# Third mixer: attention probabilities turned by a product with diag(1/sum)

## The chip, the cores and the metric

The kernel runs on one core of a Trainium2 chip. What is measured is the device time of one execution in microseconds; of several runs the median is shown. Beside it there is one execution with the hardware profiler, from which the profile and the trace come.

## What is computed

Two blocks of two layers each over 256 context tokens and 256 latent tokens of width 1024, in float32. The four mixers are, in order: gated linear attention beside softmax attention, a gated recurrence, latent attention beside retention (the third mixer, which the change touches), and a state-space scan; each is followed by a feed-forward part. The attention of the third mixer, with 8 heads:

```python
def attend(q, k, v):
    s = jnp.einsum('bqhd,bkhd->bhqk', q, k).astype(jnp.float32) * (QK_DIM ** -0.5)
    p = jax.nn.softmax(s, axis=-1).astype(v.dtype)
    return jnp.einsum('bhqk,bkhd->bqhd', p, v)

# in mla_retention_mixer: latent queries see context and latent keys, context queries the context alone
    q_c, k_c, v_c = mla_heads(z_c[..., :MLA_IN], ...)
    q_l, k_l, v_l = mla_heads(z_l[..., :MLA_IN], ...)
    a_l = blocked_attend(q_l, concat(k_c, k_l), concat(v_c, v_l))      # blocks of 128 queries
    a_c = attend(q_c, k_c, v_c)
    y = concatenate([a, r]) @ w_out                                     # r is the retention
```

## The kernel before

The program is written by hand: each engine has its own list of stages and runs through it in order, and semaphores (`wait_ge`, `then_inc`) tie them. Three helpers carry most operations, so most rows of the profile have their lines: `Pe.mm` (L169, a matmul with stationary `w` and moving `x`; `ps<-x,w` in the profile's names), `Pe.tr` (L179, TensorE's transpose, moving the identity that stands in `sb_cst`), and `Vec.tt` (L200, a product or sum of two tensors on VectorE or GpSimd). ScalarE's copies are L258, its exponentials with a row sum L253, other activations L252; VectorE's maxima are L229, its small scalings L214, reciprocals L226, scaled products L217.

The third mixer is the class `Mla`. After its projections it runs 23 steps. In each step stand side by side: one attention unit in four phases, the making of a query or key head (with its norm and its rotation) for a later unit, a part of the retention, and a part of the modulation vectors of a later stage (`mods`, with weights by DMA, `ps<-sb_slot,sb_SX`). Each engine goes through its part of a step in a fixed order, so what is queued earlier in a step holds back what is queued later.

An attention unit is two heads by 128 queries. There are 16: for each pair of heads m, c = 0 and 1 are context queries with nk = 256 keys, c = 2 and 3 latent queries with nk = 512. Unit u = 4m + c. The class `Attend` has its phases:

- TensorE, `scores` in step s: two matmuls into banks 3 and 4. VectorE, `maxima`. ScalarE, `exps`: P = exp(scale * s - max) into SBUF, with the row sums in r.
- VectorE, `norms`, later in step s: rr = 1/r, then P = P * rr, one product over both heads, 128 x 2nk elements; it signals "pn".
- TensorE, `turn`, in step s+1, head by head: waits for "pn" and for its bank, and turns the nk/128 blocks of P into bank 5 with the identity. There is one bank for the turns, so head 1 waits until ScalarE has copied head 0 to PT (`copies`). Between the two turns TensorE does `values` of the unit before.
- TensorE, `values`, in step s+2: v times PT into bank 6; ScalarE, `gather`, copies the bank after c = 3.

TensorE's order in a step is: turn of head 0, values of the older unit, turn of head 1, scores of the next unit, a part of mods, rotation, the new head's product, retention, the head's sum of squares, a part of mods. P and PT have two buffers each, chosen by u % 2. `Attend` is also used by the first mixer (`Even`), whose `st` holds P, PT, m and r.

`p.RA` is a buffer of 128 x 2048 floats. In the trace it is written by two transfers of modulation weights before 760 us and is used again by the state-space scan after 2034 us.

Of the kernel before, what the change touches and what calls it, by code (L numbers as in the profile page):

```python
# [16 lines left out]
D = 1024  # L17
# [70 lines left out]
class Events:  # L88
# [3 lines left out]
    def __init__(self, nc, ctx):  # L92
        self.nc, self.ctx = nc, ctx
        self.sems, self.n, self.at, self.bank, self.ends = {}, {}, {}, {}, {}
        self.counting = True
# [953 lines left out]
def block_load(W, c0):  # L1049

    view = lambda s: s[:, :].rearrange("p (k n) -> p k n", k=KT)
    return 4096, [(view, W[:, c0:c0 + 512].rearrange("(k p) n -> p k n", p=128))]
# [1112 lines left out]
class Attend:  # L2165
# [8 lines left out]
    def turn(self, pe, u, h):  # L2174
        p, tag = self.p, self.tag
        nk = self.units[u][1]
        b = self.tb[h % len(self.tb)]
        pe.wait_ge("pn", tag, u)
        pe.vacant(b)
        for j in range(nk // 128):  # L2180
            i = pe.tr(p.ps[b][:, 128 * j:128 * j + 128], self.st["P"][u % 2][:, h, 128 * j:128 * j + 128])
        i.then_inc(*pe.sig("tr", tag, u, h))
        pe.until(b, "pt", tag, u, 1 if len(self.tb) == 2 else h)

# [81 lines left out]
    def norms(self, dve, u):  # L2266
        tag, st = self.tag, self.st
        nk = self.units[u][1]
        P = st["P"][u % 2][:, :, 0:nk]
        r, rr = (st["r"][:, i, 2 * u:2 * u + 2] for i in range(2))  # L2270
        dve.wait_ge("p", tag, u, 1)
        dve.recip(rr, r).then_inc(*dve.sig("recip", tag, u))
        dve.wait_ge("recip", tag, u)
        dve.mul(P, P, rr.unsqueeze(2).broadcast_to([128, 2, nk])).then_inc(*dve.sig("pn", tag, u))


# [716 lines left out]
class Mla:  # L2993
# [7 lines left out]
    def __init__(self, p, mods, next_mods, before):  # L3001
        self.p, self.mods, self.more, self.before = p, mods, next_mods, before
        io = p.io
        W = io["w_in_2"][0]
        place = Place(p.room, 8192)
        self.rq, self.rk, self.rg, self.rv = (place(4, T) for _ in range(4))
        self.cq, self.ckv, self.kr = place(2, T), place(T), place(T)
        narrow = [(lambda s: s[:, :].rearrange("p (k n) -> p k n", k=KT)[:, :, 0:416], W[:, 0:416].rearrange("(k p) n -> p k n", p=128))]
        cp = lambda x, sc=1.0: [(x[:, m, :], ACT.Copy, sc) for m in range(4)]
        self.proj = Projections(  # L3010
            p, "mla.in", [block_load(W, 416), (4096, narrow)] + [block_load(W, c0) for c0 in (928, 1440, 1952)], mods,
            [("features", cp(self.rq)),
             ("narrow", [("features", 128 * m, 128, 0, self.cq[:, m, :]) for m in range(2)]
              + [("features", 256, 128, 0, self.ckv), ("features", 320, 96, 64, self.kr[64:96, :])]),
             ("features", cp(self.rk, 0.125)), ("tokens", cp(self.rv)),
             ("features", [(self.rg[:, m, :], ACT.Silu, 1.0) for m in range(4)])], ("ffn1.res", "x"), ("mla.in", "x"))

        top = place.at
        low = Place(p.room, 0, 8192)
        self.QH, self.KH = low(4, T), low(4, T)  # L3020
        self.su, (za, zb) = 1, p.slots[2:4]
        s = p.slots[self.su]
        self.tmps = [(low(T), low(T)), (s[:, 2560:3072], s[:, 3072:3584])]
        rt, self.t1 = s[:, 3584:3584 + TC], s[:, 3840:3968]
        self.wu, self.wk = s[:, 0:1536].rearrange("p (k n) -> p k n", k=2), s[:, 1536:2560]
        place = Place(p.room, top)
        P = [place(2, T), place(2, T), low(2, T), za[:, 2048:3072].rearrange("p (h n) -> p h n", h=2)]
        self.vv = low(4, T)
        st = {"P": P[0:2], "PT": P[2:4], "m": place(32), "r": place(2, 32)}
        self.kvnorm = RmsHeads(p, "kv", self.ckv, "ones", 128, T, 128, p.v("mkv_n"), self.tmps[0], 0, 3)  # L3030
        self.items, units = [], []
        for h in range(8):
            q, k = self.QH[0:96, h % 4, :], self.KH[0:96, h % 4, :]
            self.items += [(RmsHeads(p, (h, y), z, "ones", 96, T, 96, p.v(gain)[0:96], self.tmps[y], 0, 3),
                            Rope(p, (h, y), z[:, TC:T], 96, "rotM", "cosM", "sinM", rt, 0, 3))
                           for y, (z, gain) in enumerate(((q, "mqn"), (k, "mkn")))]
        for m, c in itertools.product(range(4), range(4)):
            nk = TC if c < 2 else T
            heads = [(self.QH[0:96, h % 4, 128 * c:128 * c + 128], self.KH[0:96, h % 4, 0:nk], lambda j, h=h: self.vv[:, j, 64 * h:64 * h + 64])
                     for h in (2 * m, 2 * m + 1)]  # L3040
            units.append((heads, nk, m, c, p.H[:, m, :] if c == 3 else None))
        self.attend = Attend(p, 0, units, 96 ** -0.5, st, (3, 4), (5,), 6)
        self.steps = len(units) + self.LAG + 2
        self.lg = place(6, 16)
        rt2 = place(TC)
        self.F, self.Rv = p.H[:, 7, :], p.H[:, 3, :]
        D = [za[:, 0:1024], za[:, 1024:2048], za[:, 3072:4096], place(1024)]
        self.DJ = [(d[:, 0:T], d[:, T:2 * T]) for d in D]
        self.o, self.r = zb[:, 3072:3072 + T], zb[:, 3584:3584 + T]
        self.ropes = [Rope(p, (n, m), x[:, m, TC:T], 128, "rotR", "cosR", "sinR", rt2, 0, 3) for n, x in enumerate((self.rq, self.rk)) for m in range(4)]  # L3050
        done = [("mla.lat", ("att", 0, m)) for m in range(4)] + [("mla.ret", ("mix", m)) for m in range(4)]
        order = (0, 4, 1, 5, 2, 6, 3, 7)
        self.out = OutProj(p, "mla", io["w_out_2"][0], p.H, 0, False, mods, order,
                           lambda e, k: e.wait_ge(*done[order[k]][1], of=done[order[k]][0]), free=self.place_free)
# [1428 lines left out]
```

## Time and profile before

| | before |
|---|---|
| median of 3 runs | 2423.95 us |
| lowest and highest | 2421.72, 2424.27 us |
| span of the profiled execution | 2417.1 us |
| TensorE busy | 2247.9 us, 93% |
| VectorE busy | 1490.4 us, 62% |
| ScalarE busy | 1083.1 us, 45% |
| attention steps of the third mixer | about 1476 to 1626 us of the span |

The profiled execution's own time is its span, from the first instruction to the last. Times in rows are microseconds unless marked ns. PE is TensorE's matmul, PEld its weight load, DVE VectorE, ACT ScalarE, POOL GpSimd. TensorE's matmuls are pipelined and their ends are modelled: several that follow each other overlap in the rows, so the time that one more costs is read from starts, not from durations. "issue" as the reason of an idle time means that no wait is visible.

### The profile page before, as it was taken

How to read it: one execution, taken by the hardware profiler on the slowest of the kernel's cores; microseconds unless marked ns; L12 is line 12 of the kernel's file. 1: busy time of each engine (PE TensorE's matmuls, PEld its weight loads, DVE VectorE, ACT ScalarE, POOL GpSimd, SP SyncE). 2: the span in 40 equal slices, each digit the busy share in tenths (PEclk: the TensorE clock that was granted, in tenths of full speed). 3: DMA queues.
4: the chain of work that ended last, by engine and by line, in shares of the span. 5: the costliest groups of instructions: out<-in, count | busy, mean ns of one | idle time of the engine just before them, and what ended most of it. 6: DMA issues, size and time to landing. Idle time of an engine off the chain costs nothing.

```text
span 2417.1 us, 35402 instructions
## 1 busy us (share of the span) xinstructions
PE 2247.9 (93%) x14822; PEld 1793.5 (74%) x14822; DVE 1490.4 (62%) x2379; ACT 1083.1 (45%) x1831; POOL 147.7 (6%) x185
## 2 busy tenths in 40 slices
PE   6978899999999999988999988989999999769999
PEld 3844476888886777777999863347888887759999
DVE  6448738565566477885457325555666566996454
ACT  4354446222234466655455435654332334545553
POOL 0001100000000000000000002200200201000210
PEclk8998999999999999998999999999999999989999
DMA  7263344344425465434553223432444434544543
GB/s 279 70 258 140 140 157 150 130 149 155 157 87 218 139 209 174 140 141 143 179 189 134 103 92 122 157 139 90 149 156 163 145 125 193 202 142 140 207 177 123
DMA packets 173439, 372.47 MB, mean 154 GB/s; under 512 B 7520, under 2 KB 99936, under 8 KB 158944
## 3 DMA queue, kind: packets, MB, share of 16 engines
q1 hardware_dynamic: 173280, 370.21, 43.9%
q8 instruction: 117, 1.92, 0.3%
q14 instruction: 42, 0.34, 0.0%
HBM read 339.74 MB, written 30.44 MB: 153 GB/s over the span
## 4 chain that ended last, share of the span: by engine, by line
PE 77%; DVE 12%; ACT 7%; issue 3%; DMA 2%; POOL 0%; SPq 0%; DVEq 0%; ACTq 0%; POOLq 0%
PE ps L169 75%; DVE sb_R L200 4%; ACT sb_R L252 2%; PE ps L179 1%; DMA sb_slot<-mod_w 1%; ACT sb_R L258 1%; DVE sb_H L200 1%; DVE sb_R L229 1%; DMA sb_slot<-even_w_in 1%; ACT L245 1%; DVE sb_R L232 1%; DVE sb_slot L200 1%; DVE sb_X L217 1%; DVE sb_WP L200 1%; DVE sb_R L214 1%
## 5 line engine op out<-in xcount | busy, mean ns | idle before, releaser
L169 PE MATMUL ps<-sb_HP,sb_WP 128*128 128x512 f32 (+1 forms) x5808 | 1070.5, 345 | 16.2 <-DVE sb_HP L200 9.9
L169 PEld LDWEIGHTS ps<-sb_HP,sb_WP 128*128 128x128 f32 x5808 | 915.8, 190 | 155.3 <-issue 16.5
L200 DVE TENSOR_TENSOR sb_WP<-sb_slot,sb_WP 128x1024 fp32r<-128x1024 f32 x380 | 467.7, 1236 | 554.4 <-ACT sb_WP L258 553.6
L258 ACT ACTIVATE sb_WP<-sb_slot 128x1024 fp32r<-128x1024 f32 x380 | 399.2, 1057 | 706.5 <-PE ps L169 680.7
L169 PE MATMUL ps<-sb_XP,sb_WP 128*128 128x256 f32 (+1 forms) x2976 | 499.1, 330 | 0.6 <-DVE sb_R L200 0.4
L169 PEld LDWEIGHTS ps<-sb_XP,sb_WP 128*128 128x128 f32 x2976 | 446.5, 190 | 52.3 <-DVE sb_R L200 0.9
L200 DVE TENSOR_TENSOR sb_R<-sb_R 128x256 f32<-128x256 f32 (+4 forms) x411 | 202.0, 527 | 12.9 <-ACT sb_R L252 10.0
L169 PE MATMUL ps<-sb_R 128*32 128x64 f32 (+7 forms) x1768 | 163.4, 292 | 35.8 <-issue 8.0
L169 PEld LDWEIGHTS ps<-sb_R 128*32 128x32 f32 (+3 forms) x1768 | 116.0, 157 | 74.7 <-issue 37.2
L200 POOL TENSOR_TENSOR sb_R<-sb_R 128x512 f32<-128x512 f32 (+1 forms) x82 | 91.0, 1136 | 774.8 <-ACT sb_R L252 774.8
L252 ACT ACTIVATE sb_R<-ps 128x512 f32<-128x512 f32 (+1 forms) x208 | 99.2, 513 | 79.7 <-PE ps L169 75.7
L252 ACT ACTIVATE sb_R<-sb_R 128x512 f32<-128x512 f32 (+5 forms) x127 | 83.6, 667 | 81.4 <-DVE sb_R L200 79.8
L258 ACT ACTIVATE sb_R<-ps 128x512 f32<-128x512 f32 (+4 forms) x163 | 69.6, 508 | 71.3 <-PE ps L169 61.3
L169 PE MATMUL ps<-sb_WP,sb_HP 128*128 128x512 f32 x384 | 88.4, 390 | 1.3 <-DVE sb_HP L200 1.3
L169 PEld LDWEIGHTS ps<-sb_WP,sb_HP 128*128 128x128 f32 x384 | 71.8, 188 | 17.3 <-DVE sb_HP L200 1.7
L200 POOL TENSOR_TENSOR sb_H<-sb_H 128x512 f32<-128x512 f32 (+1 forms) x15 | 18.3, 1223 | 1066.6 <-ACT sb_H L252 1066.6
L169 PE MATMUL ps<-sb_H,sb_cst 128*128 128x512 f32 (+4 forms) x178 | 61.1, 487 | 18.4 <-ACT sb_H L252 15.0
L258 ACT ACTIVATE sb_slot<-ps 128x256 f32<-128x256 f32 (+3 forms) x124 | 45.5, 397 | 61.6 <-PE ps L179 40.9
L245 ACT ACT_TABLE_LOAD x30 | 38.5, 1283 | 74.9 <-PE ps L169 56.3
L200 DVE TENSOR_TENSOR sb_XP<-sb_R,sb_XP 128x256 fp32r<-128x256 f32 (+1 forms) x116 | 70.6, 619 | 2.2 <-ACT sb_XP L258 1.6
L200 DVE TENSOR_TENSOR sb_cst<-sb_cst,sb_R 128x512 f32<-128x512 f32 (+1 forms) x112 | 69.5, 662 | 2.9 <-ACT sb_cst L252 2.4
L169 PE MATMUL ps<-sb_slot,sb_SX 128*2 128x512 f32 x472 | 61.7, 611 | 4.9 <-DMA sb_slot<-mod_w 4.9
(153 smaller groups left out, 1812.8 us busy)
## 6 DMA issues: line engine op xcount, KB each, us to landing
sb_slot<-mlp_w SPq DMA_DIRECT2D x32, 2048.0 KB, 9.0
sb_slot<-mod_w SPq DMA_DIRECT2D x14, 2048.0 KB, 8.5
sb_R<-ada_w SPq DMA_DIRECT2D x12, 2048.0 KB, 7.8
sb_slot<-ada_w SPq DMA_DIRECT2D x24, 1024.0 KB, 4.9
sb_slot<-ffn_w_gate SPq DMA_DIRECT2D x22, 1024.0 KB, 5.5
sb_slot<-ffn_w_up SPq DMA_DIRECT2D x22, 1024.0 KB, 8.5
sb_slot<-ffn_w_down SPq DMA_DIRECT2D x9, 2048.0 KB, 7.7
sb_slot<-odd_w_in SPq DMA_DIRECT2D x32, 512.0 KB, 7.5
```

What stands on the lines that cost most here:

```text
L169: return self.e.matmul(out, w, x, start=start, stop=stop, skip_group_check=True)
L179: return self.e.transpose(out, a, self.p.c("ident"))
L200: return BLANK if self.e is None else self.e.tensor_tensor(out, a, b, op)
L214: return self.e.tensor_scalar(out, a, s1, None, op0) if op1 is None else self.e.tensor_scalar(out, a, s1, s2, op0, op1)
L217: return BLANK if self.e is None else self.e.scalar_tensor_tensor(out=out, in0=a, scalar=s, in1=b, op0=op0, op1=op1)
L229: return BLANK if self.e is None else self.e.reduce_max(out, a, AX.X)
L232: return BLANK if self.e is None else self.e.tensor_tensor_scan(out, a, b, 0.0, ALU.mult, op)
L245: self.e.preload_act_table_set(t)
L252: return self.e.activation(out, a, func, bias=bias, scale=scale)
L258: return self.e.activation(out, a, ACT.Copy) if scale is None else self.e.activation(out, a, ACT.Copy, scale=scale)
```

## The change

`Mla` gives its `Attend` two more buffers D of 128 x 2 x 128 floats, in `p.RA`. Where `st` has "D", `norms` leaves P as it is and writes D, for each head the 128 x 128 identity times rr, a diagonal matrix of 1/sum. `turn` multiplies P's blocks, as the stationary operand, with this diagonal matrix as the moving one, in a normal f32 matmul, in place of the transpose with the identity. The result in bank 5 is the same: normalised P, turned. Before it writes D of unit u, VectorE waits for the turns of unit u-2. The first mixer's attention has no "D" and stays as it was.

```diff
@@ Attend.turn
         for j in range(nk // 128):
-            i = pe.tr(p.ps[b][:, 128 * j:128 * j + 128], self.st["P"][u % 2][:, h, 128 * j:128 * j + 128])
+            o, P = p.ps[b][:, 128 * j:128 * j + 128], self.st["P"][u % 2][:, h, 128 * j:128 * j + 128]
+            i = pe.mm(o, P, self.st["D"][u % 2][:, h, :], True, True) if "D" in self.st else pe.tr(o, P)
         i.then_inc(*pe.sig("tr", tag, u, h))
@@ Attend.norms
         dve.recip(rr, r).then_inc(*dve.sig("recip", tag, u))
         dve.wait_ge("recip", tag, u)
+        if "D" in st:
+            if u >= 2:
+                dve.wait_ge("tr", tag, u - 2, 1)
+            eye = self.p.c("ident").unsqueeze(1).broadcast_to([128, 2, 128])
+            dve.mul(st["D"][u % 2], eye, rr.unsqueeze(2).broadcast_to([128, 2, 128])).then_inc(*dve.sig("pn", tag, u))
+            return
         dve.mul(P, P, rr.unsqueeze(2).broadcast_to([128, 2, nk])).then_inc(*dve.sig("pn", tag, u))
@@ Mla.__init__
-        st = {"P": P[0:2], "PT": P[2:4], "m": place(32), "r": place(2, 32)}
+        DD = [p.RA[:, 256 * i:256 * i + 256].rearrange("p (h n) -> p h n", h=2) for i in range(2)]
+        st = {"P": P[0:2], "PT": P[2:4], "D": DD, "m": place(32), "r": place(2, 32)}
```

## Rows read from the trace of the kernel before

**Rows 1.** The page: span, TensorE's busy time, granted clock in 40 slices (tenths).
```profile
span 2417.1 us, 35402 instructions
...
PE 2247.9 (93%) x14822; PEld 1793.5 (74%) x14822; DVE 1490.4 (62%) x2379; ACT 1083.1 (45%) x1831; POOL 147.7 (6%) x185
...
PEclk8998999999999999998999999999999999989999
```

**Rows 2.** Windows: the attention steps and the stage behind (length, busy times, clock, DMA).
```profile
1476.00:1626.00 150.00, 133.50 (x727) 56.39 (x723) 85.19 (x174) 82.97 (x176) 24.79 (x60) 0.98 0.43 148
1626.00:1800.00 174.00, 171.90 (x748) 139.80 (x747) 106.75 (x141) 67.71 (x94) 27.98 (x20) 1.00 0.37 130
```

**Rows 3.** TensorE's groups by form, 1476 to 1626 us (count, busy us, mean ns, idle before).
```profile
L179 PE MATMUL ps<-sb_cst,sb_R 128*128 128x128 f32 x96 | 18.3, 302 | 9.6 <-DVE sb_R L200 6.6 <-ACT sb_R L258 1.9 <-ACT sb_slot L258 0.9
L169 PE MATMUL ps<-sb_R 96*128 96x512 f32 x32 | 15.9, 621 | 0.0
```

**Rows 4.** VectorE's groups by form, 1475 to 1622 us.
```profile
L200 DVE TENSOR_TENSOR sb_R<-sb_R 128x1024 f32<-128x1024 f32 x8 | 9.8, 1225 | 0.3
...
L200 DVE TENSOR_TENSOR sb_R<-sb_R 128x512 f32<-128x512 f32 x8 | 5.5, 692 | 0.3
...
L200 DVE TENSOR_TENSOR sb_R<-sb_R,sb_cst 96x256 f32<-96x256 f32 x12 | 4.9, 411 | 0.0
...
L226 DVE RECIPROCAL sb_R<-sb_R 128x2 f32<-128x2 f32 x16 | 2.6, 161 | 6.3 <-ACT sb_R L253 6.3
```

**Rows 5.** Timeline of TensorE: second-head turns and what follows (start, us).
```profile
1513.60 0.66 PE L179 MATMUL ps<-sb_cst,sb_R 128*128 128x128 f32 x4
1514.10 1.03 PE L169 MATMUL ps<-sb_R 96*128 96x256 f32 x4
...
1562.70 0.44 PE L179 MATMUL ps<-sb_cst,sb_R 128*128 128x128 f32 x2
1562.97 1.03 PE L169 MATMUL ps<-sb_R 96*128 96x256 f32 x4
```

**Rows 6.** f32 products on 128 columns elsewhere: timeline, then the group's mean.
```profile
176.22 1.16 PE L169 MATMUL ps<-sb_R 64*128 64x128 f32 x8
...
966.96 1.05 PE L169 MATMUL ps<-sb_R 128*128 128x128 f32 x8
967.76 2.35 PE L169 MATMUL ps<-sb_HP,sb_WP 128*128 128x256 f32 x12
...
L169 PE MATMUL ps<-sb_cst 128*128 128x128 f32 x160 | 19.3, 276 | 0.0
```

**Rows 7.** The chain that ended last, 1470 to 1630 us (start, us, what).
```profile
1482.55 0.44 PE ps L179 x2
...
1557.45 0.69 DVE sb_R L200
...
1595.86 0.69 DVE sb_R L200
...
1609.19 1.24 DVE sb_R L200
...
1622.36 0.59 PE ps L179 x4
```

**Rows 8.** Timeline: the first turn of unit 0 and its copy.
```profile
1481.64 0.44 PE L179 MATMUL ps<-sb_cst,sb_R 128*128 128x128 f32 x2
...
1482.12 0.38 ACT L258 ACTIVATE sb_R<-ps 128x256 f32<-128x256 f32 x1
```

**Rows 9.** Windows of TensorE (length, busy, granted clock, DMA).
```profile
1608.00:1609.00 1.00, 0.00 (x0) 0.68 0.00 0
...
1615.00:1616.00 1.00, 1.00 (x3) 0.90 0.00 0
```

**Rows 10.** Timeline of TensorE: first turns of units 14 and 15.
```profile
1610.47 1.12 PE L179 MATMUL ps<-sb_cst,sb_R 128*128 128x128 f32 x4 [3.83 <-DVE sb_R L200]
...
1620.68 0.66 PE L179 MATMUL ps<-sb_cst,sb_R 128*128 128x128 f32 x4 [1.73 <-DVE sb_R L200]
```

## Prediction, made before the changed kernel was run

> **What bounds the kernel now.** I read four views, in this order. First the page: the span is 2417.1 us and TensorE is busy for 93% of it, at full clock in nearly every slice [rows 1]. The median of the runs shown is 2423.95 us, so 6.85 us lie outside the profiled span (or in the spread of 2.5 us between the runs shown); I take them as fixed and add the change to the median. Second, the stage: attention units of the third mixer run from 1476 to 1626 us. There TensorE is busy 133.5 us of 150, VectorE 85.2 and ScalarE 83.0 [rows 2]. So this stage has 16.5 us without TensorE work, and the stage behind it (171.9 of 174) has next to none: time lost here isn't given back there. Third, the groups of instructions: the 96 turns (TensorE's transposes, L179) and VectorE's products that normalise P [rows 3, 4]. Fourth, the chain of work, which says which of these durations reach the end. From 1500 to 1593 us it is mostly TensorE itself, interrupted once per step by maximum, exponential, copy and square; the product with 1/sum lies on it only where no other item fills the wait: once in the middle, and in the last four units [rows 7]. That is the view on which the sum hangs.
>
> **What the change removes and adds.** The first mixer's Attend has no "D" in its st, so only these 16 units change: eight with 256 keys ("half": 2 blocks of 128 per head) and eight with 512 ("full": 4 per head), two heads each, 96 blocks in all.
>
> *VectorE.* The product with P takes 1.225 us for a full unit and 0.692 for a half one [rows 4]. In its place comes one product of 128x256, whatever the unit. The trace has no product of that shape from these operands; the nearest row is 0.411 us (96x256, SBUF only) [rows 4]. Bounds: 0.16 us, what the reciprocal of two columns takes, and 0.69, the row of twice the width [rows 4]. I take 0.41, since cost follows the columns over all three rows. So a full unit gets 0.81 us shorter, a half one 0.28: 8 x 0.81 + 8 x 0.28 = 8.7 us of VectorE's time. On the chain are two full products (1609.19, and 1619.40 like it) and three half ones (1557.45, 1595.86, and 1602.15 like it) [rows 7]: 2 x 0.81 + 3 x 0.28 = 2.5 us gained. The other 6.2 us were beside TensorE's work and bring nothing: the turn asks for P a step later, when the product is long done. By the ends of the bound the gain is 1.1 or 3.7 us.
>
> *TensorE.* A product of f32 operands is two MATMUL records: scores of eight full units and two heads are 16 calls and show as x32, while 96 turned blocks show as x96 [rows 3]. So each block goes from one MATMUL to two, and each weight load likewise. Occupation before: a full turn (4 records) starts at 1513.60 and the next group at 1514.10, so 0.50 us; a half turn (2) 1562.70 to 1562.97, so 0.27 [rows 5]. Occupation after: the trace has f32 products of the very shape, 128x128 weights on 128 columns. Eight of them take 1.05 us from first start to last end; less the 0.28 us of one, 0.77/7 = 0.110 us a record [rows 6]. Upper bound: x8 in 1.16 with 64 rows gives 0.88/7 = 0.126. Lower bound: from the eight's start to that of the group behind them, 0.80/8 = 0.10 [rows 6]. I take 0.11. A full turn is then 8 x 0.11 = 0.88, +0.38 us; a half turn 4 x 0.11 = 0.44, +0.17.
>
> *How many of them are on the chain.* Of the 32 turns, 28 stand in the chain: 15 of 16 full ones and 13 of 16 half ones; first and last are shown [rows 7]. The other four are the first heads of units 0, 1, 2 and 12, whose copy finds ScalarE busy. For unit 0 that cover is thin: the turn ends at 1482.08 and its copy begins at 1482.12 [rows 8], so 0.13 of its 0.17 comes through. The sum: 15 x 0.38 + 13 x 0.17 + 0.1 = 5.7 + 2.2 + 0.1 = +8.0 us. All of it is before scores in TensorE's order, so that maximum, exponential, head square and everything behind them start later by as much; the bubble in front of the head sums stays as it is. There is one bank (5) for the turns, so within a unit the second head waits for the copy of the first: with the first turn longer, values of the older unit, which stand between, start later too, and hide nothing of it.
>
> *The new wait.* VectorE waits for the turn of unit u-2 before it writes D. In program order that turn is behind it by more than a step; ScalarE's exponentials of unit u already wait for it, and they come before this product. It costs nothing. No DMA and no queue is touched; RA isn't used by anything else in this stage. The copies of PT, of the same size, stay.
>
> **The clock.** After the scores of unit 14 TensorE is idle for 3.83 us, until the normalised P is there [rows 10]. In that gap its granted clock falls from 2.4 to 1.2 GHz (0.68 in the slice from 1608 to 1609) and comes back only after 1615 [rows 9]. Work from 1610.47 to about 1615.2, 4.7 us, is at half clock: 2.4 us lost. With a shorter VectorE product the gap becomes 3.0 us. If the low stretch stays as long as it was, 0.81 us more of it fall on work, +0.4 us. If it does not come, the change is better by 2.4 us instead.
>
> The Trainium skill ("TensorE: Matmul & The Clock Gate", Part 4) says that transposes don't count as activity for the clock in the way matmuls do; products in their place would then help to keep the clock up. The trace neither shows nor excludes it: with turns in every step of this stage the clock stays at full but for the one idle gap. It speaks for the second rival and changes nothing in the sum.
>
> **The sum.** 8.0 - 2.5 + 0.4 = +5.9 us: 2423.95 + 5.9, so 2429.8 us.
>
> **Rivals.**
>
> 1. *Products cost more than their nearest shape.* At 0.126 us a record a full turn takes 1.01 (+0.51) and a half one 0.50 (+0.23): 15 x 0.51 + 13 x 0.23 + 0.2 = 10.8; less 2.5, plus 0.4: +8.7, 2432.7 us. For it: these turns now run at (0.66 - 0.28)/3 = 0.13 a record [rows 5], wider than the 0.11 of f32 products, so something about this place may space them. Against: the x8 row, in the middle of another mixed stream. At the lower bound of 0.10 the sum is 15 x 0.30 + 13 x 0.13 + 0.1 - 2.1 = +4.2, 2428.2 us.
>
> 2. *The clock doesn't fall any more* (not slower by what can be told). It decides from the point at which the idle gap before unit 14's turn is too short for the drop; the stage has a gap of 1.73 us without a drop and one of 3.83 with it [rows 10], and 3.0 lies nearer to the latter. Time: 8.0 - 2.5 - 2.4 = +3.1, so 2427.1 us. Whether the drop comes may also change from run to run, which the 2.5 us between the runs shown would allow.
>
> 3. *A turn and a product cost the same*, if the turn's records were paced by something that a product shares. Then only VectorE's gain is left: -2.5 + 0.4 = -2.1, and with the clock kept -4.9 us, 2419.1 to 2421.9. Against it: two records for one [rows 3], and 0.11 x 2 is well over 0.125.
>
> 4. *The product costs four times the turn.* By rows: a block takes 0.125 us now (0.50/4) and would take 0.50; 15 x 4 + 13 x 2 = 86 blocks x 0.375 = 32 us, less 2.5: +30, 2454 us. The rows of f32 products contradict it by more than a factor of two. The rule behind this rival is the Trainium skill's: "Perfetto Trace Analysis" (Transposes) asks for transposes rather than standard matmuls, and the table of terms in "TensorE: Matmul & The Clock Gate" calls transpose mode four times faster for FP32. By the rows here the direction holds and the factor would be 1.8.
>
> That VectorE's time becomes visible as a gain of its full 8.7 us is no case: it was idle for 65 of 150 us in this stage.
>
> **How the numbers follow.** About 0.2% (4.85 us) is what a measurement of this kernel can tell from no change. Forecast (+5.9, with an error of about 1.5 us of its terms and of the two medians): 0.54, of which 0.14 falls under 4.85. Rival 1: 0.16. Rival 2: 0.23, all within 0.2% but little. Rival 3: 0.04, of which 0.01 is faster by over 0.2%. Rival 4: 0.02. Something else, either way: 0.01. Slower: 0.40 + 0.16 + 0.02 + 0.01 = 0.59; same: 0.14 + 0.23 + 0.03 = 0.40; faster: 0.01. The range reaches from rival 2 less the spread of medians (2427.1 - 1.6) to rival 1 and some tenths (2433.5): 2425.5 to 2433.5, and leaves out rivals 3 and 4 and the worst ends of both sides.
>
> **What would show it.** In the profile of the changed kernel: no L179 from P in this stage but 192 records of L169 with 128*128 weights from sb_R on 128 columns of sb_RA; eight of them in about 1.05 us (1.16 for rival 1, 2.0 for rival 4), four in 0.6. The 128x256 product on VectorE, 16 times, near 0.41 us. The stage from its first turn to its last 5 to 6 us longer, grown by 0.76 us in every full step and 0.34 in every half one from the third on, while the last two full units grow by no more than a few tenths, since 0.81 comes back there. The idle before unit 14's turn 3.0 instead of 3.83 us, and PEclk beside it tells rival 2. I am wrong if full steps in the middle grow by less than half of the 0.76 (then something hid the turns), or if a product that isn't on the chain above turns out to be on it.

## The result, and the profile after

The changed kernel takes 2429.01 us (median of 6 runs, 2427.52 to 2430.97), the kernel before 2421.45 (median of 6, 2417.02 to 2424.27). The ratio is 1.0034, with a 95% interval of 1.0024 to 1.0044: slower by 7.6 us. The forecast was 2429.8 us and +5.9. The time came out close with the help of a second miss, and that was luck: the sum started from a median of 2423.95, and three more runs brought it down to 2421.45. The loss itself was forecast 1.7 us too small by the medians, and 3.9 too small by the traces; 2423.95 plus the 9.75 us of the traces below would be 2433.7, past the upper end of the range.

The page of the changed kernel, to be read beside [rows 1]: span, busy times, granted clock in 40 slices.

```profile
span 2426.8 us, 35594 instructions
...
PE 2261.6 (93%) x14918; PEld 1808.0 (75%) x14918; DVE 1482.2 (61%) x2379; ACT 1084.0 (45%) x1831; POOL 147.6 (6%) x185
...
PEclk8998899999999999999999999999999999889999
```

TensorE has 96 instructions more and 13.7 us more of busy time, VectorE 8.2 us less: the change does what it says. The span grew by 9.7 us. To find where, I took the start of each of the 32 turns in both traces, counted from the first turn of unit 0, and subtracted. From that turn to the first matmul of the output projection (`ps<-sb_HP,sb_WP`) there are 144.17 us before (1481.64 to 1625.81) and 153.92 after (1483.66 to 1637.58): +9.75. The changed trace is 2.0 us late when this stretch begins and gets 2.1 us back behind it, in stages that the change doesn't touch. That is of the size by which runs of one kernel differ (7 us between the lowest and highest of before), so the stretch is the measure from here on. The growth in it, where a turn starts, in us (a turn is hidden where it grows and the next one does not start later):

| at the start of | growth | since the row above: what the steps are |
|---|---|---|
| unit 2, head 0 | 0.82 | half turns, 0.27 to 0.28 each; one hidden |
| unit 4, head 0 | 2.32 | full turns, 0.50 each; one hidden |
| unit 6, head 0 | 3.41 | four half turns |
| unit 8, head 0 | 5.01 | 0.50 each, one only 0.36; VectorE gives 0.26 back |
| unit 10, head 0 | 6.10 | four half turns |
| unit 12, head 0 | 8.10 | four full turns |
| unit 14, head 0 | 7.59 | three half turns, +0.82, one hidden; -1.33 of VectorE's |
| unit 14, head 1 | 8.55 | a full turn at half clock: 0.96 |
| unit 15, head 0 | 8.55 | a full turn, the clock, -0.81 of VectorE's |
| projection | 9.75 | two full turns, 1.0, and 0.19 of a wait for ScalarE |

Summed by causes: 14 full turns at 0.50 and one at 0.36, 13 half ones at 0.27 and unit 0's first at 0.28 make +11.2. VectorE's shorter product gives 0.26 (unit 8), 0.26 (12), 0.27 (13), 0.80 (14) and 0.81 (15), less the 0.19 that unit 15 loses again: -2.2. The clock costs +0.77 more than before (0.46 in unit 14's first turn and 0.31 up to unit 15, where the growth was 0.00 and 0.50 - 0.81 is -0.31). 11.2 - 2.2 + 0.8 = 9.8.

TensorE's and VectorE's groups by form of the changed kernel, 1470 to 1640 us (count, busy us, mean ns, idle before), answering [rows 3, 4].

```profile
L169 PE MATMUL ps<-sb_RA,sb_R 128*128 128x128 f32 x192 | 31.5, 303 | 6.6 <-DVE sb_RA L200 4.7 <-ACT sb_R L258 0.9 <-ACT sb_slot L258 0.7
...
L200 DVE TENSOR_TENSOR sb_RA<-sb_cst,sb_R 128x256 f32<-128x256 f32 x16 | 6.8, 425 | 0.5
```

The 128x256 product takes 0.425 us for the 0.411 I took. The mean of one MATMUL record, 303 ns against 302 before, tells nothing of its price: records overlap. The price stands in the starts. Timeline of TensorE, second-head turns of units 3 and 8 with what follows (start, us), the same places as [rows 5], and a turn in unit 2:

```profile
1517.44 1.16 PE L169 MATMUL ps<-sb_RA,sb_R 128*128 128x128 f32 x8
1518.44 1.03 PE L169 MATMUL ps<-sb_R 96*128 96x256 f32 x4
...
1570.00 0.71 PE L169 MATMUL ps<-sb_RA,sb_R 128*128 128x128 f32 x4
1570.55 1.03 PE L169 MATMUL ps<-sb_R 96*128 96x256 f32 x4
...
1500.43 1.10 PE L169 MATMUL ps<-sb_slot,sb_cst 96*96 96x512 f32 x2 [1.38 <-ACT sb_slot L252]
1501.36 1.06 PE L169 MATMUL ps<-sb_RA,sb_R 128*128 128x128 f32 x8
```

From its start to that of the next group a second-head turn is 1.00 us where it was 0.50 (full), and 0.55 where it was 0.27 (half), where I had 0.88 and 0.44. First-head turns, which have another group behind them, grow by the same 0.50 and 0.27, from 0.59 to 1.09 and from 0.37 to 0.64; so it is the growth that is the same everywhere, and the factor of two only in the second heads. In unit 2's first turn, behind `96*96` products, the eight records take 1.06 us, the 1.05 of my row [rows 6], and so they do in unit 7's first, behind `128*128` ones. In all other full turns at full clock they take 1.16: behind `128*64` products, as the one at 1517.44, and in first heads behind `128*2` ones (weights of 64 or 2 columns). Within all these groups the records start 0.11 us apart, (1.06 - 0.28)/7; in the longer ones 0.10 more goes by between the first record and the second. The transposes paid 0.06 there (0.66 against 0.60 us for four), so a full turn grows by four records, 0.45, and 0.04 of a dearer start.

The clock around unit 14, windows and timeline of the changed kernel, answering [rows 9, 10]:

```profile
1619.00:1620.00 1.00, 0.00 (x0) 0.80 0.00 0
1620.00:1621.00 1.00, 0.92 (x4) 0.50 0.00 0
...
1626.00:1627.00 1.00, 1.00 (x3) 0.79 0.00 0
```
```profile
1620.08 2.08 PE L169 MATMUL ps<-sb_RA,sb_R 128*128 128x128 f32 x8 [3.03 <-DVE sb_RA L200]
...
1631.25 1.16 PE L169 MATMUL ps<-sb_RA,sb_R 128*128 128x128 f32 x8 [0.93 <-DVE sb_RA L200]
```

The idle gap is 3.03 us, the forecast's 3.0, and in it the granted clock still falls from 2.4 to 1.2 GHz. In this pair of executions the low stretch has the same length: from 1619.6 to 1626.4 after, 1608.4 to 1615.2 before (a window at 0.80 has 0.4 us of half clock in it). Of it 6.3 us now fall on work, where it was 4.7.

What became of VectorE's last gain shows ScalarE's timeline around unit 15's first copy (the last row):

```profile
1630.91 1.06 ACT L258 ACTIVATE sb_WP<-sb_slot 128x1024 fp32r<-128x1024 f32 x1
1631.86 1.15 ACT L258 ACTIVATE sb_HP<-sb_H 128x512 fp32r<-128x512 f32 x2
1632.90 0.60 ACT L258 ACTIVATE sb_slot<-ps 128x512 f32<-128x512 f32 x1
```

The first turn of unit 15 ends at 1632.41, but ScalarE still prepares the projection (WP, HP) and copies at 1632.90. The chain that ended last says the same: it leaves TensorE here and goes through these pieces.

```profile
1631.03 0.94 ACT sb_WP L258
1631.97 1.03 ACT sb_HP L258 x2
1633.01 0.50 ACT sb_slot L258
```

### The profile page after: what moved, and what is told of

Its sections match the earlier page's. It is cut to its first block, busy times and chain, and to the rows that moved or that the text cites. A ratio compares the mean times of both kernels' runs of the same rounds, so it can differ in the third digit from the quotient of the medians.

```text
span 2426.8 us, 35594 instructions
## 1 busy us (share of the span) xinstructions
PE 2261.6 (93%) x14918; PEld 1808.0 (75%) x14918; DVE 1482.2 (61%) x2379; ACT 1084.0 (45%) x1831; POOL 147.6 (6%) x185
## 4 chain that ended last, share of the span: by engine, by line
PE 77%; DVE 12%; ACT 7%; issue 2%; DMA 2%; POOL 0%; SPq 0%; DVEq 0%; ACTq 0%; POOLq 0%
PE ps L169 76%; DVE sb_R L200 4%; ACT sb_R L252 2%; DMA sb_slot<-mod_w 1%; ACT sb_R L258 1%; DVE sb_H L200 1%; PE ps L179 1%; DVE sb_R L229 1%; DVE sb_WP L200 1%; ACT L245 1%; DVE sb_slot L200 1%; DVE sb_R L232 1%; DMA sb_slot<-even_w_in 1%; DVE sb_X L217 1%; DVE sb_R L214 1%
## 5 line engine op out<-in xcount | busy, mean ns | idle before, releaser
L200 DVE TENSOR_TENSOR sb_R<-sb_R 128x256 f32<-128x256 f32 (+4 forms) x395 | 186.7, 509 | 12.3 <-ACT sb_R L252 10.0
```

What stands on the lines that cost most here:

```text
L200: return BLANK if self.e is None else self.e.tensor_tensor(out, a, b, op)
```

## Theory, rivals and the experiments

Theory A: the loss is TensorE's alone. A record costs 0.11 us whether it is a transpose's or a product's; a product has two; a group of products pays 0.10 more at its start behind nearly all of its neighbours, a group of transposes 0.06. VectorE's gain is real but mostly beside the chain. The rivals: D as an operand, rather than the product as such, makes the turns slow (B); the swap pays where VectorE stands on the chain, and loses only because it is made everywhere (C); the clock, not the turns, makes the loss (D).

All lengths below are of the same stretch: 144.17 before, 153.92 after. A drop is a stretch in which the granted clock is halved. Each kernel has one trace, and the drops differ from execution to execution. Six of the twelve traces, but neither of these two, have one of 3.4 us in unit 2, worth 0.65 us with the short turns and 1.05 with the long ones. The drop at unit 14 is 6.8 us long in four (before, changed, experiments 2 and 7), where it begins 1.7 to 2.6 us after TensorE went idle, and 3.4 us in four (experiments 1, 3, 4 and the split of 6), where it begins 2.7 to 4.5 us after that; the same gap of 3.03 us is in both groups. So I say for each which drops it had, and read growths turn by turn. Medians stand beside those kernels that were run several times, each against the kernel before on its chip (2420.7 or 2421.6 us there).

**1. VectorE's part alone.** D is written, P stays as it is, and the turns are transposes with the identity; so the division by the sum is left out.

```diff
 # the changed kernel's Attend.turn
-            i = pe.mm(o, P, self.st["D"][u % 2][:, h, :], True, True) if "D" in self.st else pe.tr(o, P)
+            i = pe.tr(o, P)
```

> VectorE's half of the change alone: D is written as in the changed kernel, but the turns are transposes with the identity again, so the attention is left without its division by the sum. The stage, from the first turn to the first matmul of the output projection, takes 144.2 us in the kernel before and 153.9 in the changed one. Theory (VectorE's saving counts only where its product is on the chain): 0.28 saved in units 8, 12 and 13, 0.81 in 14 and up to 0.81 in 15, so the stage gets 2.5 us shorter, 141.7, with the clock's drop in the gap before unit 14 as before; the time about 2419 against 2421.5. Rival A (VectorE's time was never on the chain, other waits stand behind it): 144.2. Rival B (the drop of the clock goes with the shorter gap): 139.3.

Measured: 2416.7 us (median of 10), ratio 0.9989 [0.9978, 1.0000]; the stretch 142.76, -1.41. It contains two things of the clock: +0.65 of a drop in unit 2, and -0.33 since the low stretch at unit 14 is half as long. It begins 1.4 us behind the end of the idle gap here, while TensorE is working (timeline, then windows):

```profile
1609.85 0.66 PE L179 MATMUL ps<-sb_cst,sb_R 128*128 128x128 f32 x4 [3.03 <-DVE sb_RA L200]
```
```profile
1610.00:1611.00 1.00, 1.00 (x12) 1.00 0.00 0
1611.00:1612.00 1.00, 0.90 (x6) 0.64 0.00 0
```

Without the two the stretch is 1.7 us shorter: -0.27 in unit 8 and in each half unit of 12 and 13, -0.80 in 14, -0.81 in 15, the same as in the changed kernel, but then 0.69 are lost again instead of 0.19. TensorE's timeline, both turns of unit 15:

```profile
1618.92 0.66 PE L179 MATMUL ps<-sb_cst,sb_R 128*128 128x128 f32 x4 [0.93 <-DVE sb_RA L200]
...
1621.22 0.66 PE L179 MATMUL ps<-sb_cst,sb_R 128*128 128x128 f32 x4 [0.62 <-ACT sb_slot L258]
```

The second turn waits 0.62 us for ScalarE's copy. With products the first turn is 0.50 longer and covers most of that wait. Of the 8.2 us that VectorE does less, 1.7 reach the end.

**2. TensorE's part alone.** P is normalised by VectorE as before, and turned by a product with the identity (the condition on the scale leaves the first mixer as it was).

```diff
 # the kernel before, Attend.turn (o, P: bank and block)
-            i = pe.tr(o, P)
+            i = pe.mm(o, P, p.c("ident"), True, True) if len(self.units) == 16 and self.scale != 0.125 else pe.tr(o, P)
```

> TensorE's half alone: VectorE normalises P as before, and the turns are f32 products with the identity in place of transposes. Theory (28 to 30 of 32 turns on the chain, 0.50 us for a full one and 0.27 for a half one, as the changed kernel's trace shows): 15 x 0.50 + 14 x 0.27 = 11.3 us, plus 0.5 to 1 us for turns at half clock: stage 155.9 to 156.5 us, time about 2433. Rival (the dearer group start of 0.1 us in the changed kernel comes from D as an operand written late, not from the product): full turns +0.38, half ones +0.17, stage 152.5.

Measured: 2429.66 us (median of 4), ratio 1.0046 [1.0028, 1.0064]; the stretch 156.36, +12.19. TensorE's timeline, a full and a half turn:

```profile
1512.02 1.16 PE L169 MATMUL ps<-sb_cst,sb_R 128*128 128x128 f32 x8
...
1522.78 0.71 PE L169 MATMUL ps<-sb_cst,sb_R 128*128 128x128 f32 x4
```

The same 1.16 and 0.71 with the identity as with D, and the same 0.50 and 0.27 from turn to turn: rival B falls. Of 12.19, 1.05 is a drop in unit 2 and -0.06 the clock at unit 14, so the turns alone are +11.2. Up to unit 14's second turn the growths of this kernel, less 1.05, and of the changed one differ by VectorE's gains (10.24 - 1.05 - 7.59 = 1.60 at unit 14, and 0.27 + 0.26 + 0.27 + 0.80 is 1.60). So the two parts add, except for the 0.5 us of experiment 1: 11.2 - 1.7 = 9.5 against 9.75 - 0.77 = 9.0.

**3. Each product made twice.** The price of a record by itself.

```diff
-            i = pe.mm(o, P, self.st["D"][u % 2][:, h, :], True, True) if "D" in self.st else pe.tr(o, P)
+            for _ in range(2 if "D" in self.st else 1):
+                i = pe.mm(o, P, self.st["D"][u % 2][:, h, :], True, True) if "D" in self.st else pe.tr(o, P)
```

> The changed kernel with every block's product made twice, into the same place: 16 records in a full turn and 8 in a half one. It asks how the price of a turn splits. In the changed kernel a half turn behind a column-tiled group takes 0.55 us until the next group starts and a full one 1.00, so 4 records more cost 0.45. Theory A (0.1125 us a record and 0.10 for the start of the group): full 1.00 + 8 x 0.1125 = 1.90, half 1.00. Theory B (the price per record is 0.125, as I get by dividing 1.00 by 8): full 2.00, half 1.05 to 1.10. Theory C (the second product of the same block is cheaper, since its weights are there): below 1.8. The stage grows by 15 x 0.90 + 15 x 0.45 = 20 us on 153.9 by A, less what the waits for ScalarE cover: 173 to 174.

Measured (one run): 2454.36 us, the stretch 173.03. Timeline of TensorE, a full turn and a half one, each with what follows:

```profile
1523.22 2.05 PE L169 MATMUL ps<-sb_RA,sb_R 128*128 128x128 f32 x16
1525.11 1.03 PE L169 MATMUL ps<-sb_R 96*128 96x256 f32 x4
...
1534.88 1.16 PE L169 MATMUL ps<-sb_RA,sb_R 128*128 128x128 f32 x8
1535.87 1.03 PE L169 MATMUL ps<-sb_R 96*128 96x256 f32 x4
```

Eight more records make 1.00 into 1.89 us, four more make 0.55 into 0.99: 0.11 each, and the 0.10 at the start comes once. Turn by turn, against the changed kernel, 14 full turns grow by 0.89 and 14 half ones by 0.45; unit 15's first grows by 0.71, since it now covers the wait for ScalarE's copy, and the first turns of units 2 and 12, hidden until now, come out with 0.56 and 0.41: together 20.4. The stretch grew by only 173.03 - 153.92 = 19.1, because its low clock at unit 14 is half as long, which takes 1.3 off (0.25 more in unit 14's first turn, 1.57 less behind it). Timeline and windows there:

```profile
1639.24 3.51 PE L169 MATMUL ps<-sb_RA,sb_R 128*128 128x128 f32 x16 [3.03 <-DVE sb_RA L200]
```
```profile
1638.00:1639.00 1.00, 0.00 (x0) 0.96 0.00 0
1642.00:1643.00 1.00, 1.00 (x11) 0.83 0.00 0
```

The price of a record is settled, by the starts; that the expected 173 to 174 came out is partly the shorter drop.

**4. The swap in the last four units only** (rival C). The kernel before, with D and the products for u of 12 and more.

```diff
-            i = pe.tr(o, P)
+            i = pe.mm(o, P, self.st["D"][u % 2][:, h, :], True, True) if "D" in self.st and u >= 12 else pe.tr(o, P)
 # Attend.norms: the block that writes D
-        if "D" in st:
-            if u >= 2:
+        if "D" in st and u >= 12:
+            if u >= 14:
```

> D and the product only for units 12 to 15, in which VectorE's product is on the chain in every unit; the other twelve as in the kernel before. Theory: seven or eight turns on the chain cost 3 x 0.27 + 4 x 0.50 and 0.5 to 1 more for those at half clock, together 3.3 to 3.8; VectorE gives back 0.26 + 0.28 + 0.81 + 0.5: 1.9. Stage 1.4 to 1.9 us longer than before: 145.6 to 146.1. Rival (where the product is on VectorE's chain the swap pays): 144.2 or less.

Measured (one run): 2419.12 us, the stretch 145.07, +0.90, where 145.6 to 146.1 was expected. 0.65 of it came in unit 2 by a drop. The remaining +0.25 has a low stretch at unit 14 of half the length: from unit 12's first turn to the projection it grows by 0.24 where the changed kernel grows by 1.65, and the whole difference lies between 14 and 15, behind the gap. Freed of the clock the changed kernel's growth there is 1.65 - 0.77 = 0.9, which the terms give too: 4 x 0.50 + 3 x 0.27 = 2.8 of turns, less 1.9 of VectorE's. So even where VectorE stands on the chain a full unit pays two turns, 1.00 us, for 0.81, and rival C isn't supported. That my expectation missed is the clock's doing, which the next runs take up.

**5. The gap before unit 14 filled** (rival D). The changed kernel, with work for TensorE that nobody reads, put ahead of unit 14's turn: three f32 products of 512 columns, or twenty transposes.

```diff
             if t1 == 14:
                 _, spare = e.take(0, 3)
+                for _ in range(3):
+                    e.mm(spare[:, :], self.p.c("ident"), self.p.c("distF"), True, True)
 # the other kernel instead
+                for _ in range(20):
+                    e.tr(spare[:, 0:128], self.p.c("ident"))
```

> The changed kernel, with three f32 products of 512 columns (2.6 us at full clock) in TensorE's idle gap of 3.03 us before unit 14's turn; their result is not read. Theory: the clock doesn't fall there, the 6.1 us of work that ran at 1.2 GHz run at 2.4, and the stage gets 3 us shorter: 150.9 instead of 153.9. Rival (the drop is a matter of something before the gap): stage 153.9 with the low stretch where it was.

> The changed kernel, with twenty transposes of 128x128 (2.3 us at full clock) in the same gap. If transposes keep the clock up like products: stage 150.9 us and no drop. If they don't count as work for the clock: the clock falls as it did or sooner, stage 153.9 or a little more. I hold both for equally likely; the stage before and behind is full of products.

Measured (one run each): with products 2422.73 us, the stretch 151.13 and no low clock in it; with transposes 2426.71 us, the stretch 152.19, of which 1.06 is a drop in unit 2. TensorE's windows in the gap of the kernel with transposes, and its timeline:

```profile
1617.00:1618.00 1.00, 1.00 (x12) 1.00 0.04 16
1618.00:1619.00 1.00, 0.68 (x7) 1.00 0.00 0
1619.00:1620.00 1.00, 0.64 (x5) 1.00 0.00 0
```
```profile
1616.27 2.40 PE L179 MATMUL ps<-sb_cst 128*128 128x128 f32 x20
1619.36 1.16 PE L169 MATMUL ps<-sb_RA,sb_R 128*128 128x128 f32 x8 [0.68 <-DVE sb_RA L200]
```

The granted clock stays at 1.00 (2.4 GHz) through the filled gap with either filler, and from unit 14 to the projection the two kernels grow alike (-0.64 and -0.63). The Trainium skill ("TensorE: Matmul & The Clock Gate", Part 4) says that transposes don't engage the clock as matmuls do. This run doesn't show that: in its one execution twenty transposes held the clock up as three products did, while it fell at this place in all eight traces without filler. The drop cost the changed kernel 2.79 us. Without it the change still costs 151.13 - 142.14 = 9.0 us (142.14 is the kernel before with the same filler, next), so the clock explains 0.8 of 9.75 in this pair of traces, and rival D falls as the main cause.

**6. The kernel before, with the gap filled, and with the norms split.** Can the kernel before be made faster at the same place? The first takes the same three products. The second has VectorE normalise P head by head, so that each turn waits for its own head alone. The third has both, with the split in the last four units only.

```diff
 # Attend.turn; `and u >= 12` in the third kernel
-        pe.wait_ge("pn", tag, u)
+        pe.wait_ge("pn", tag, u, *((h,) if self.scale != 0.125 and u >= 12 else ()))
 # Attend.norms
+        if self.scale != 0.125 and u >= 12:
+            for h in range(2):
+                dve.mul(P[:, h, :], P[:, h, :], rr[:, h:h + 1].broadcast_to([128, nk])).then_inc(*dve.sig("pn", tag, u, h))
+            return
```

> The kernel before, with the three unread products of 512 columns in TensorE's gap of 3.83 us before unit 14's turn. Theory: the clock doesn't fall there, and the 4.7 us of work that ran at half clock run at full: stage 144.17 - 2.4 = 141.8 us; the time 1.5 to 2.4 us lower on average, about what five rounds can just tell. Rival (the drop only moves to the next gap, before unit 15's turn, or to the third unit): stage 142.5 to 144.

> The kernel before, with the product that normalises P made head by head, and each head's turn waiting for its own. No TensorE work is added. Theory: where the product is on the chain the first turn starts half of it sooner: 0.3 in units 8 and 13 at most, 0.55 in 14 and 15, 0.1 of which goes on a second instruction's fixed cost: stage 1.2 to 1.5 us shorter than before, 142.7 to 143.0; the time moves by less than can be told. Rival: head 1's turn then waits for its own product or for ScalarE's copy, and the stage stays within 0.3 of 144.2.

> The same filler, and the product that normalises P made head by head in units 12 to 15 alone, each head's turn waiting for its own; no other unit pays for the second wait. Theory: from the shifts of the head-by-head kernel, 0.3 in unit 13, 0.55 in 14 and 0.55 in 15, of which ScalarE's preparations take back 0.5: stage 1.0 us below that with the filler alone, 140.8 (no drop of the clock), and the time 3 us below that of the kernel before. Rival: the second product's start and wait cost what the first saves, 141.8.

Measured: filled alone 2418.67 us (12 runs), ratio 0.9986 [0.9974, 0.9997], the stretch 142.14. Split alone 2419.28 (10 runs), ratio 0.9995 [0.9984, 1.0006], 143.34. Both 2417.1 (12 runs), ratio 0.9982 [0.9973, 0.9992], 142.16 with a drop in unit 2 of 0.65. Read turn by turn, the split alone loses 0.49 us by unit 11, in steps of up to 0.10: each unit has one wait more on TensorE and one product more on VectorE, and gains nothing there; that is why the third kernel has it in the last four units alone. There it first loses 0.15 in unit 12, then gives 0.3 in unit 13 and 0.55 in unit 14; in unit 15 a gain of the same size is lost again (+0.5). Of the 0.83 us by which the split alone is shorter, 0.6 are the clock's, whose low stretch at unit 14 is half as long in this trace; without that only 0.2 are left, far from the 1.2 to 1.5 that were expected and within the 0.3 of its rival. The third kernel is 4.5 us below the kernel before on its chip, 0.18%; against the filler alone it is 1.6 us lower, which the two intervals don't tell apart. In the stretch, without unit 2's drop, it has 2.66 us less than before, 2.03 of them the filler's. It was expected at 140.8 and has 142.16, or 141.5 without unit 2's drop.

**7. ScalarE's preparation moved.** Is it this that takes back the gain of unit 15? The changed kernel, with the HP parts of the projection's preparation prepared later.

```diff
-    EARLY = ((0,), (0, 1)), ((1,), (2, 3)), ((2,), (4, 5))
+    EARLY = ((0,), ()), ((1,), (0, 1, 2, 3)), ((2,), (4, 5))
```

> The changed kernel, with ScalarE's and VectorE's first two input blocks of the output projection prepared one step later, behind the copies of unit 15's turns in place of ahead of them. It asks why unit 15's second turn starts 2.30 us after its first, where unit 11's takes 2.11 and before the change it took 1.61 (and 2.30 again with VectorE's half alone). Theory (ScalarE's 1.06 + 1.15 us of preparation stand in front of the copy and eat what VectorE gave back): from first to second turn 2.1 us or a little less, 0.2 gained here; with transposes it would be 0.69. The output projection then starts up to 1.2 us later, since the blocks are ready later: stage 153.7 to 155. Rival (the spacing comes from TensorE's own work between the turns): 2.30 stays. The drop before unit 14 may last 3.4 or 6.8 us in any run; the spacing of unit 15 is behind it.

Measured (one run): 2429.46 us. TensorE's timeline of unit 15 and the projection:

```profile
1628.32 1.16 PE L169 MATMUL ps<-sb_RA,sb_R 128*128 128x128 f32 x8 [0.92 <-DVE sb_RA L200]
1629.41 1.09 PE L169 MATMUL ps<-sb_R 128*64 128x128 f32 x16
1630.43 1.16 PE L169 MATMUL ps<-sb_RA,sb_R 128*128 128x128 f32 x8
...
1636.80 3.46 PE L169 MATMUL ps<-sb_HP,sb_WP 128*128 128x512 f32 x8 [1.77 <-DVE sb_HP L200]
```

From turn to turn 2.11 us instead of 2.30: the 0.19 came from there. But TensorE now stands idle for 1.77 us in front of the projection, waiting for HP, and the projection starts 6.37 us after the second turn instead of 4.03, 2.3 later. So the stretch has 157.11, or 156.0 without a drop in unit 2. The mechanism is confirmed; as a remedy it costs 2.1 us in the stretch, and my expectation of 153.7 to 155 had at most 1.2 for that delay.

## Why the prediction held, and where it didn't

- *TensorE is the bound, and what is added to it reaches the end.* Right: nothing of the turns' time comes back in the stretch, and I had 28 of 32 turns on the chain. The 28 are the ones that grew (one by 0.36 instead of 0.50, unit 7's first: it grew by 0.46 itself, and the kernel before had waited 0.1 us behind it), and with them unit 0's first, by 0.28 where I let 0.13 through. The first heads of units 1, 2 and 12 were hidden as said.
- *The price of a product.* The term that was mis-sized: +0.38 and +0.17 forecast, +0.50 and +0.27 measured. 14 x 0.12 + 13 x 0.10 and the 0.2 of unit 0 make the 3.2 us between 8.0 and 11.2. The mis-sized step is the choice of the row at 966.96: its eight records stand behind another `128*128` group, while nearly all of these turns stand behind `128*64` or `128*2` products and pay 0.10 more at their start, which eight times 0.11 leaves out. The row with that start stood there too (176.22, 1.16 us), as did the warning of rival 1, that transposes here ran wider than the x8 row. I priced old turns from starts in their place, which holds the start of the group, and new ones from the spacing within a group elsewhere, which doesn't. Rival 1 (10.8 of turns, 11.2 measured) was the better account of TensorE's number, but by a record of 0.126 us throughout, where the runs have 0.11 and a dearer start.
- *VectorE.* -2.5 forecast, -2.2 measured, with every unit right (0.27 and 0.81 at 8, 12 to 15). What I left out was who is next behind unit 15's turn: ScalarE, 0.19 us.
- *The clock.* The drop stayed, so rival 2 fell. The gap was forecast to 0.03 us. The term was +0.4 and came to +0.77 in this pair of traces: 1.6 us more of the low stretch falls on work, half of it because the gap is 0.8 shorter and half because the clock fell 2.5 us after the gap's start instead of 1.7. My term had the first half only. Neither number is firm: experiment 4 has the same gap of 3.03 us with a low stretch of half the length, and grows by 1.4 us less there, which would turn the term to about -0.6. That it was small beside the turns was right; its sign is open.
- *The new wait for the turn of unit u-2* costs nothing that the trace shows: D's product waits 0.5 us in all 16 units together.
- *Rivals 3 and 4.* A turn and a product don't cost the same, and the factor in second heads is 2, not 4: 0.50 to 1.00 us, where 4 would have been 2.0. The factor of four that rival 4 takes from the Trainium skill ("TensorE: Matmul & The Clock Gate", table of terms) has its direction right here, and its size isn't borne out.
- *The signs.* From unit to unit a full step in the middle grew by 1.00 us where I had 0.76, a half one by 0.55 where I had 0.34. Unit 14's step grew by 0.96 and unit 15's by 1.19, where I had a few tenths: the turns cost more, the clock took more, and ScalarE kept 0.19. The stage grew by 9.75, not by 5 to 6.
- *The base.* I put 6.85 us between median and span. The changed kernel's profiled execution has 2428.54 us with a span of 2426.8: 1.7 lie outside. The rest was spread, which this kernel has of itself (2415.5 to 2427.0 us over all runs of before).

Open: why the clock falls in unit 2 in some executions and not in others, where the idle time is the same 1.39 us.

## What to carry to other kernels

Where TensorE bounds a stage, moving work to it from an engine that idles is likely to lose. Price the new instruction by its count of records at the very place, from start to start, with the neighbour that it has there. A gain on the other engine counts only in the units in which it stands on the chain, and only until the next engine that is late. An idle gap in which the clock falls costs more than its length: unread work in it gained 2.0 us in the stretch here, while with a gap shortened by 0.8 us the clock still fell. Compare two traces turn by turn, and look at the low stretches of each first: a sum over the whole stretch can come out right for the wrong reason, as in experiment 3.

## What the runs showed of the hardware

- Two f32 MATMUL records for one product of 128x128 on 128 columns, 0.11 us each; one for a transpose, also 0.11. Behind `128*64`, `128*2` and `64*128` products a group starts 0.10 us dearer than behind `96*96` or `128*128` ones if it is of products (1.16 against 1.06 us for eight records, 0.71 against 0.61 for four), and 0.06 (0.44 against 0.38 us for two) if it is of transposes. Why is open.
- The granted clock fell to half at the gap of 3.0 to 3.8 us before unit 14 in all eight traces without filler, in five of them within the gap and in three up to 1.4 us behind its end. In unit 2 it fell behind a gap of 1.39 us in six of twelve traces; the kernel before has the same gap without a drop. This is the timeline of the first experiment, in which the clock is low from 1498.6 to 1502.1:

```profile
1497.92 1.35 PE L169 MATMUL ps<-sb_slot,sb_cst 96*96 96x512 f32 x2 [1.39 <-ACT sb_slot L252]
1499.06 1.06 PE L179 MATMUL ps<-sb_cst,sb_R 128*128 128x128 f32 x4
1500.05 1.12 PE L169 MATMUL ps<-sb_slot,sb_R 128*64 128x128 f32 x8
```

  So my "1.73 us without a drop, 3.83 with one" drew no line between gaps that are safe and gaps that aren't. A drop is worth 0.65 to 2.8 us here, as much as the effects sought.
- Transposes in the gap held the clock as well as products did, in one execution each.
